# Moving the pooling mix between the q and k products, and two key transposes per pass onto the matmul engine

## The reference

```python
def _pool_mix(u, buf, start_pos, w_group, scale):      # branch A
    ...
    for gi, w in enumerate((2, 4, 8, 16)):             # 4 channel groups
        ...
        outs.append((hi - lo) / cnt - uf[:, :, sl])    # trailing mean minus token
    pooled = jnp.stack(outs, axis=2).astype(u.dtype)
    mixed = jnp.einsum('btgc,gcd->btgd', pooled, w_group)
    return mixed.reshape(u.shape) * scale, ...

def step(S, inp):                                      # branch B, one chunk, per head
    qc, kc, vc, gc = inp
    b = jnp.cumsum(gc, axis=2)
    qe = qc * jnp.exp(b); ke = kc * jnp.exp(-b)
    att = jnp.where(mask, jnp.einsum('bhik,bhjk->bhij', qe, ke), 0.0)
    o = jnp.einsum('bhik,bhkv->bhiv', qe, S) + jnp.einsum('bhij,bhjv->bhiv', att, vc)
    S = jnp.exp(b_last)[..., None] * S + jnp.einsum('bhjk,bhjv->bhkv', kc * jnp.exp(b_last - b), vc)

def _layer(x, ...):
    h = _rmsnorm(x, g_mix)
    u, q, k, v, og, zr, ga, gb = jnp.split(h @ w_in, IN_SPLIT_IDX, axis=-1)
    y_a = pool_out @ w_pool_proj                       # branch A
    y_b = (rmsnorm(o) * silu(og)) @ w_gla_proj         # branch B
    x = x + (sigmoid(ga) * y_a + sigmoid(gb) * y_b) @ w_out
    h2 = _rmsnorm(x, g_ffn)
    x = x + (silu(gate) * up) @ w_ffn_out              # inner width 2816
y = _rmsnorm(x, g_final)
```

## Time and profile before

| | |
|---|---|
| median of 3 executions | 901.15 us (900.64 to 901.22) |
| profiled execution, whole | 901.29 us |
| its span, slowest core (core 0) | 900.2 us (all cores 896.3 to 900.2) |
| PE busy (share of the span) | 875.1 us (97%) |
| DVE, ACT, POOL busy | 438.6, 261.0, 128.3 us |
| mean granted TensorE clock by core | 0.998 to 0.999 |
| PE's share of the chain that ended last | 91% |

### The profile page before, as it was taken

The page is one execution under the profiler, slowest core; times in us unless marked ns, Lnnn a source line. Parts: engine busy times, 40 slices in busy tenths (PEclk is TensorE's granted clock), DMA queues, the critical chain, the costliest instruction groups (busy, mean ns, idle before and its releaser), DMA issues.

```text
span 900.2 us, 14507 instructions; the slowest of 8 cores (896.3 to 900.2 us)
## 1 busy us (share of the span) xinstructions
PE 875.1 (97%) x4888; PEld 447.7 (50%) x4888; DVE 438.6 (49%) x715; ACT 261.0 (29%) x515; POOL 128.3 (14%) x242
## 2 busy tenths in 40 slices
PE   4999999999999999999999999999999999999996
PEld 2544566654664566456644444444444444444443
DVE  4689565657435322433267664565651331232146
ACT  4563533223322123012226614332231011101123
POOL 4535112002100000100022001120120000000002
PEclk9999999999999999999999999999999999999999
DMA  8984842749709824943695994353774844352504
GB/s 208 219 167 78 118 75 38 127 98 157 129 24 180 171 34 84 166 92 68 110 173 171 214 203 72 59 90 44 132 114 62 135 88 68 55 113 47 94 24 164
DMA packets 57116, 100.50 MB, mean 112 GB/s; under 512 B 41538, under 2 KB 42178, under 8 KB 49748
## 3 DMA queue, kind: packets, MB, share of 16 engines
q0 software_dynamic: 10336, 66.75, 43.5%
q1 hardware_dynamic: 46564, 32.63, 15.3%
q10 hardware_dynamic: 144, 0.20, 0.1%
HBM read 139.36 MB, written 11.53 MB: 168 GB/s over the span
## 4 chain that ended last, share of the span: by engine, by line
PE 91%; DMA 4%; DVE 2%; issue 1%; ACT 1%; POOL 0%; DVEq 0%; POOLq 0%; ACTq 0%; SPq 0%
PE ps L422 87%; DMA ring<-w_f 1%; DMA ring<-w_a 1%; DVE R L319 1%; DMA R<-R 1%; PE ps L765 1%; PE ps L829 1%; DVE R L323 1%; DMA xres<-xm 0%; PE ps L407 0%; PE ps L746 0%; PE ps L766 0%; ACT R L315 0%; PE ps L540 0%; PE ps L723 0%
## 5 line engine op out<-in xcount | busy, mean ns | idle before, releaser
L422 PE MATMUL ps<-hT,ring 128*128 128x368 bf16 (+2 forms) x2720 | 506.5, 343 | 3.0 <-DVE qeZ L323 1.1
L422 PEld LDWEIGHTS ps<-hT,ring 128*128 128x128 bf16 x2720 | 260.5, 98 | 230.3 <-issue 7.9
L313 ACT ACTIVATE sgt<-ps 128x368 f32<-128x368 f32 (+2 forms) x207 | 109.6, 530 | 432.7 <-PE ps L422 381.2
L422 PE MATMUL ps<-ring,R 128*128 128x512 bf16 (+2 forms) x1028 | 222.5, 377 | 0.0
L319 DVE TENSOR_TENSOR R<-ps,sgt 128x368 bf16<-128x368 f32 (+1 forms) x110 | 66.1, 601 | 237.1 <-PE ps L422 229.7
L422 PEld LDWEIGHTS ps<-ring,R 128*128 128x128 bf16 (+1 forms) x1028 | 101.3, 99 | 118.3 <-issue 1.2
L319 DVE TENSOR_TENSOR xres<-xres,ps 128x512 f32<-128x512 f32 (+2 forms) x103 | 69.7, 680 | 66.2 <-PE ps L422 66.0
L422 PE MATMUL ps<-R,ring 128*128 128x368 bf16 (+1 forms) x320 | 70.6, 343 | 0.0
L315 ACT ACTIVATE R<-xres 128x1024 bf16<-128x1024 f32 (+3 forms) x45 | 45.8, 1018 | 83.3 <-DVE xres L323 43.4
L186 POOL DMA_DIRECT2D ring<-w_f x34 | 18.6, 549 | 294.4 <-PE ps L422 292.8
L422 PE MATMUL ps<-ring,hT 128*128 128x512 bf16 (+1 forms) x272 | 60.3, 379 | 0.0
(11 more groups left out here) (113 smaller groups left out, 443.9 us busy)
## 6 DMA issues: line engine op xcount, KB each, us to landing
ring<-w_f POOLq DMA_DIRECT2D x30, 1024.0 KB, 11.9
ring<-w_a POOLq DMA_DIRECT2D x24, 1024.0 KB, 12.3
y_p<-xres SPq DMA_DIRECT2D x15, 512.0 KB, 2.8
xres<-xp POOLq DMA_DIRECT2D x8, 512.0 KB, 12.3
R<-xp SPq DMA_DIRECT2D x8, 512.0 KB, 6.6
xres<-xp SPq DMA_DIRECT2D x8, 512.0 KB, 31.2
ring<-w_f POOLq DMA_DIRECT2D x4, 768.0 KB, 11.9
R<-sgla SPq DMA_DIRECT2D x2, 1024.0 KB, 10.6
```

The source lines that it names most:

```text
L313: T.op('act', lambda e: e.activation(out=out, in_=in_, func=func, scale=scale, bias=bias), reads=rd, writes=wr)
L422: return [(lambda e, k=k: e.matmul(out, lhsT=lw(k), rhs=rx(k), start=(k == 0), stop=(k == K - 1))) for k in range(K)]
```

## The change

Three things. The eight mixes of blocks A and B leave their place behind the q and k products: after each of block B's four products, one channel group is mixed for A and B, and a cost of 0.44 is yielded; in pass 0 the four mixes of S follow, all before the gate products. The release of the ring buffer of q and k comes after all of it. Units 0 and 1 of each pass get their row-major k by two TensorE transposes and an ACT copy in `sA1`, as S does; block A's DMA transposes cover units 2 and 3 only. At the end, each of the last unit's sums has a cell of 32 bytes of its own in `gst` (columns 0, 8, 16) and POOL's results go to `stat` (columns 0, 8, 16); and `final` of unit 6 is called after `final_w` of unit 7, no longer inside the split.

```diff
@@ qk, L579
                     if blk != 'S':
                         u0 = c0 // 128
-                        xpose(keTM[:, u0:u0 + 4, c * 128:(c + 1) * 128], keT[:, c, c0:c0 + 512])
+                        if u0 == 0:
+                            xpose(keTM[:, 2:4, c * 128:(c + 1) * 128], keT[:, c, 256:512])
+                        else:
+                            xpose(keTM[:, u0:u0 + 4, c * 128:(c + 1) * 128], keT[:, c, c0:c0 + 512])
@@ gla, sA1, L728
-                if isS:
+                if isS or u < 2:
                     bt = nbank()
                     pt = banks_b[bt]
                     pe([(lambda e, c=c: e.transpose(out=pt[0:r, c * 128:(c + 1) * 128], in_=keT[:, c, c0:c0 + r], identity=ident_b[:, :]))
@@ dense1, L950
-            yield from qk(rq, 'B')
+            for g, cost in enumerate(qk(rq, 'B')):
+                yield cost
+                for b_ in (['A', 'B'] if has_s else ['A', 'B']):
+                    pool_mix(b_, g)
+                yield 0.44
             slab_release(j_qk)
-            for b_ in ['A', 'B']:
+            if has_s:
                 for g in range(4):
-                    pool_mix(b_, g)
-                yield 0.87 * BLK[b_][1] / 512
+                    pool_mix('S', g)
+                yield 0.2
             j0, r0 = next_slab('a', 4)
             jp, rp = next_slab('a', 5)
             if has_s:
-                yield from gate('a', 0, r0, rp, cols[:1])
-                for i_, cost in enumerate(gate('a', 0, r0, rp, cols[1:2])):
-                    if i_ < 4:
-                        pool_mix('S', i_)
-                    yield cost
-                yield from gate('a', 0, r0, rp, cols[2:])
+                yield from gate('a', 0, r0, rp, cols)
@@ final_q, final_l, final_w, L1162
-                act(junk[:, c0_:c0_ + n], xt, AF.Square, scale=1.0 / 32.0, accum=gst[:, k:k + 1])
+                act(junk[:, c0_:c0_ + n], xt, AF.Square, scale=1.0 / 32.0, accum=gst[:, 8 * k:8 * k + 1])
...
-                T.op('pool', lambda e: e.tensor_scalar(out=gst[:, 4:5], in0=gst[:, 0:1], scalar1=gst[:, 1:2], scalar2=EPS,
-                                                       op0=ALU.add, op1=ALU.add), reads=[gst[:, 0:2]], writes=[gst[:, 4:5]])
+                T.op('pool', lambda e: e.tensor_scalar(out=stat[:, 0:1], in0=gst[:, 0:1], scalar1=gst[:, 8:9], scalar2=EPS,
+                                                       op0=ALU.add, op1=ALU.add), reads=[gst[:, 0:1], gst[:, 8:9]], writes=[stat[:, 0:1]])
...
-                T.op('pool', lambda e: e.tensor_scalar(out=gst[:, 5:6], in0=gst[:, 2:3], scalar1=gst[:, 4:5], scalar2=None, op0=ALU.add),
-                     reads=[gst[:, 2:3], gst[:, 4:5]], writes=[gst[:, 5:6]])
-                r_ = gst[:, 6:7]
-                tt(r_, gst[:, 5:6], negh[:, 0:1], ALU.pow, eng='pool')
+                T.op('pool', lambda e: e.tensor_scalar(out=stat[:, 8:9], in0=gst[:, 16:17], scalar1=stat[:, 0:1], scalar2=None, op0=ALU.add),
+                     reads=[gst[:, 16:17], stat[:, 0:1]], writes=[stat[:, 8:9]])
+                r_ = stat[:, 16:17]
+                tt(r_, stat[:, 8:9], negh[:, 0:1], ALU.pow, eng='pool')
@@ the last group's loop, L1214
                         final_q(u, 2, 768, 256)
-                        final(pend.pop(0))
                         pend.append(u)
                         continue
...
                 if p == 1:
-                    final_w(pend.pop(0))
+                    final_w(pend.pop(1))
+                    final(pend.pop(0))
```

## The result

The changed kernel takes 903.4 us against 901.26 of the kernel before on the same chip: ratio 1.0023, 95% interval 1.0015 to 1.003, slower by 2.1 us. The forecast was 901.1, its range ended at 902.5.

A forecast was written before the change was run, and what follows sets the result against it. TensorE, busy for 97% of the span, was taken as the bound, so only its pauses could be won. Core 0: -2.35 + 1.55 + 0.7 = -0.1 against 901.29, 901.05 at the median; predicted 901.1, range 899.5 to 902.5.

The forecast's parts named there:

- Pass 1: Start of pass 1: DMA wait 1.6 and ACT waits 1.0 go, transposes add 0.25; gain 2.35 on core 0, 1.2 on core 3.
- the walk: Pass 0, block B's first product to first gate product: new order followed bank by bank with DVE's read times; cost 1.55 us.
- Rival 1: Pass 0: DVE does not hold TensorE; 899.3 if half of the 3.6 pauses goes, 897.5 if all; chance 0.14.
- The later ring loads: Pass 0, POOL: loads behind S's `sR` issued some 8 us later, needed only some 22 us on; priced at nothing.
- The end: After the last matmul: earlier square wins 0.5, but unit 6's 512 KB DMA lands at 900.84, not 900.15; cost 0.7.
- Rival 2: The end costs nothing, since unit 6's DMA finds empty engines and lands sooner than 2.7; 899.9 us, chance 0.12.
- core 0 stays slowest: Whole kernel: core 6 has the same waits and is 0.6 us ahead, so core 0 still sets the end.
- my sum of -0.1: Core 0, whole kernel: -2.35 for pass 1, +1.55 for pass 0, +0.7 for the end, against 901.29 us.
- Rival 3: Later in pass 1: ring loads or another core eat the gain; 903.4, or 902.2 with 1.2 left; chance 0.07.
- Rival 4: Pass 0: more pauses drop TensorE's clock from 2.4 to 1.2 GHz; one spell makes 903.4 us; chance 0.03.
- Rival 5: Pass 1: a DMA wait remains in front of unit 0's state product; given no chance of its own.
- The rule that I weighed against TensorE's transposes: Some 275 ns per 128x128 transpose: eight cost 2.2 us, not 0.5, the sum 1.7 higher; set aside for S's row.

The follow-up runs named there:

- the run with pass 1 alone: Pass 0 and the end's order as before, pass 1 and the sums' cells as changed, against the kernel before: 899.96 us, ratio 0.9976.
- a run a few instructions away: The change, with pass 0's two mixes behind block B's first product moved behind the second: 908.39 us.
- the three faster versions: Pass 0 and end order as before, pass 1 as changed: 0.9976 of the kernel before; plus early SP waits: 0.9979; plus DVE's long scaling cut in two: 0.9968.

## Why the prediction was wrong

**Pass 1, sum right, its split wrong.** Predicted -2.35 on core 0 and -1.2 on core 3; measured -2.29 and -1.14. But I split it into 1.6 for TensorE's transposes and 1.0 for the mixes; alone they are worth 0.35 and 1.68 (means of the cores). The mixes between the products take away both waits, since they are TensorE's work while the DMA is on its way and give ACT its time; the transposes take away only the DMA's, and what they win TensorE mostly waits for ACT.

**Pass 0, the walk right, its sum too small.** It had pauses of 0.35, 1.2, 0.55 and 1.5, 3.6 together, from start to start; counted so the measured ones are 0.34, 1.2, 0.66 and 1.6, 3.8 together (the profile's 3.17 begin at the listed ends, which take in the drain). The second product was forecast 3.70 behind the first and came 3.72 behind it, S's third mix 15.47 and came 15.59. Rival 1, that DVE does not hold TensorE, is refuted. The gate came 15.95 behind the first product and not 15.56: the chain of small products, square, reduction and masked copy lost only some 0.1, the other 0.27 stands between S's third mix and the gate, 0.36 where I had 0.09. And I let the pass win 0.14 behind the stretch, since S's mixes are missing there; it lost 0.31 instead. A new wait for DVE of 0.28 near 155 us is in it on every core, a wait near 120 on core 1, and some 0.1 stays open. The term was +1.55 and is +2.40 (2.09 + 0.31), the largest miss of the sum. Its bounds ended at 1.9: they held every handover 0.1 later, but nothing behind the stretch. The later ring loads, which I priced at nothing because TensorE needs them only much later, have another reader: the transpose of S lands behind them, and DVE waits for it. In the profiled change that cost next to nothing, in the run of the same pass 0 with SP's waits put last 0.5 in the mean. With S's mixes in the gate all of pass 0 costs 1.1 and not 2.40 (13.92 + 369.55 against 13.86 + 368.53); so S's place makes 1.3 of it.

**The end, the step that failed in kind.** I had the 512 KB DMA land 7.9 behind the last matmul (900.84 on core 0, whose last matmul ended at 892.94), and it landed 7.9 behind it, by luck to the tenth: it was issued 0.2 sooner than I had it and took 0.2 longer. I took the landing for the end of the program. It is not: SP still has 13 of its fifty serial waits to go through, 0.65. The term was +0.7 and is +1.27, and this is the whole difference, as the run with these waits put last shows (7.97). The sentence "lands 2.7 on: 900.84, where the last one landed at 900.15" compared two landings, and before there was only 0.1 between landing and end because the list had been running for 2.4 us already. Of the order itself, the earlier square is worth a little more than the 0.5 that I gave it: ACT's DMA is issued 0.6 sooner. Rival 2, the end costs nothing, is refuted.

**The core that sets the end.** I wrote that core 0 stays slowest. On core 0 my sum of -0.1 met -1.0, since its start (-0.94) and its later waits (-1.42) fell well. Core 6 went from 899.6 to 902.0. Rival 3, that the gain of pass 1 is given back, has 903.4 as its number but not its cause: the gain of pass 1 is kept, in the run with pass 1 alone it shows as 0.24% of the time. What follows in the pass costs 0.34 more in the mean (0.4 to 0.6 in the three faster versions), too little for that rival, which wanted 1.8. Rival 4 did not happen in the change, though a run a few instructions away shows its mechanism. Rival 5 is refuted, no DMA wait is left.

So: -1.72 for pass 1 (mean of the cores), +2.40 for pass 0, +1.27 at the end, and +0.6 of start and later waits that differ from run to run: 2.56 in the mean of the cores, 2.1 in the medians. Against the mean, my sum of -0.1 is off by 2.66: 0.85 in pass 0, 0.57 at the end, 0.63 because I took core 0's gain in pass 1 for all cores, and 0.61 of start and later waits, for which I had no term. Three steps failed, then: pass 0's term was too small, the end's took a landing for the end, and the sum was made for core 0, whose gain in pass 1 the others don't have. The rule that I weighed against TensorE's transposes (the Trainium skill, TensorE: Matmul & The Clock Gate, Part 4, some 275 ns each) gets no support as a price in a dense stream: a pair stands 0.11 ahead of the next mix (541.59 to 541.70).

## What to carry to other kernels

Where banks go round in a fixed turn and a slower engine empties them, putting one more user into the turn moves every later one to another bank; walk the turn with the reader's times, down to the smallest user, and change the order first in the pass where that reader is not behind. When a load moves, look at every transfer that will now share its time, and at who waits for that one. This program ends when its last queue has gone through its waits, not when the last transfer lands: put the waits on the last transfers last. (Starting the list early won nothing in the old order; in the new one it was not tried.) Before a wait is priced, ask what work another part of the change puts in front of it: two cures for one gap don't add.

## What the runs showed that I had not expected

In this case a wait on a semaphore that is long due costs SP 0.05 us; fifty are 2.4 us, of which 0.63 stood on the path here.

A one-column addition on POOL takes 0.29 when DVE rests, 0.99 when it falls 0.45 into a DVE scaling of 1024 columns, 0.45 with one of 512.

Neighbouring cores seem to take from each other. At about 665 us each core loads 1 MB of weights, and before, the four cores that wait for it (1.0 to 1.3 us, at about 678) are the four slowest. Before, core 1 issued it 2.0 ahead of core 0, and had it in 8.6 us; core 0 needed 11.1 and waited 1.00. POOL's issue and the median time to landing, core 1 and then core 0:

```profile
665.27 1.16 POOL L186 DMA_DIRECT2D ring<-w_f  x2 [0.27 <-PE ps L422]
...
ring<-w_f POOLq DMA_DIRECT2D x1, 1024.0 KB, 8.6
```

```profile
667.30 1.16 POOL L186 DMA_DIRECT2D ring<-w_f  x2 [0.27 <-PE ps L422]
...
ring<-w_f POOLq DMA_DIRECT2D x1, 1024.0 KB, 11.1
```

It is so in all four pairs of neighbours before (cores 0 and 1, 2 and 3, and so on: 8.6 to 9.6 for the first, 11.1 to 11.4 for the second). In the change the cores of two pairs are 0.3 to 0.5 apart and need 10.7 to 11.3; both of each pair wait. In the other two pairs they are 0.7 and 1.4 apart, and only the second waits. A stretch that is made equally long on all cores, as the change does with pass 1, brings neighbours closer together, and may so give part of its gain back. The three faster versions fit it (346.5 to 346.7 from the gate of pass 1 to the last matmul, 346.11 before), two others with the same pass 1 do not (346.09 and 346.24). So it is argued from these rows and was not tried by itself.
